# Bias tables of the dilated heads: built one pair ahead on ScalarE and GpSimd, in two buffers

## The reference

```python
DILATED_PATTERNS = ((128, 1), (512, 4), (2048, 16))
slopes = exp2(-8 * arange(1, 9) / 8)                      # head h: 2 ** -(h + 1)
for window, dilation in DILATED_PATTERNS:
    bias = -slopes[:, None, None] * (dilation * abs(delta))[None]
    s = where(mask, q @ k + bias, NEG_INF)
    m = max(s); e = exp(s - m); den = sum(e); num = e @ v
...                                                       # the three patterns are joined by exp(m - max m)
return sum(scale * num) / sum(scale * den)
```

## Time and profile before

| | us |
|---|---|
| median of 3 runs | 3123.47 |
| lowest and highest | 3121.69, 3126.23 |
| the profiled execution | 3126.64 |
| its span (first to last instruction) | 3124.9 |

### The profile page before, as it was taken

One profiled execution on the slowest core, in us unless ns is written; L12 is line 12 of the kernel. 1 busy time (PEld: TensorE's weight loads), 2 busy tenths in 40 slices (PEclk: granted clock), 3 DMA queues, 4 the chain that ended last, 5 costly groups with the idle time before them and its releaser, 6 DMA issues.

```text
span 3124.9 us, 42430 instructions
## 1 busy us (share of the span) xinstructions
PE 2933.4 (94%) x16328; PEld 2234.8 (72%) x16328; DVE 1830.8 (59%) x2574; ACT 915.4 (29%) x1660; POOL 1136.6 (36%) x661
## 2 busy tenths in 40 slices
PE   7999999999999999999999999999998567999998
PEld 6888867677888878887676778887796566555443
DVE  7766685756666676667757566666526985112112
ACT  3222232543222232223235422223236652111111
POOL 3444354454443444442544444443433550000000
PEclk9999999999999999999999999999999688999999
DMA  5222222013222222222200132222230004999998
GB/s 203 95 87 101 81 81 82 2 42 121 84 98 101 81 101 101 95 86 81 108 35 1 68 115 101 91 90 99 81 122 1 21 1 165 414 423 422 424 422 339
DMA packets 44789, 411.47 MB, mean 132 GB/s; under 512 B 4960, under 2 KB 5216, under 8 KB 11744
## 3 DMA queue, kind: packets, MB, share of 16 engines
q1 hardware_dynamic: 44496, 408.03, 33.6%
q0 software_dynamic: 144, 1.38, 0.1%
HBM read 407.29 MB, written 2.10 MB: 131 GB/s over the span
## 4 chain that ended last, share of the span: by engine, by line
PE 78%; DVE 10%; DMA 5%; issue 3%; ACT 3%; POOL 1%; SPq 0%; DVEq 0%; ACTq 0%; POOLq 0%
PE banks L1598 10%; PE banks L1597 10%; PE banks L1596 10%; PE banks L1561 5%; PE banks L1430 5%; PE banks L1869 5%; PE banks L1607 5%; PE banks L1608 5%; PE banks L1609 5%; DMA experts<-moe_w 4%; PE banks L1509 3%; PE banks L1880 2%; PE banks L1645 2%; PE banks L1658 2%; PE banks L1673 2%
## 5 line engine op out<-in xcount | busy, mean ns | idle before, releaser
L784 POOL TENSOR_TENSOR ffn_parts<-ring,ffn_parts 128x2048 fp32r<-128x2048 f32 x87 | 403.0, 4633 | 738.5 <-ACT ffn_parts L887 738.5
L2172 DVE SCALAR_TENSOR_TENSOR x<-banks,x 128x512 f32<-128x512 f32 x704 | 474.3, 690 | 302.2 <-PE banks L1609 301.1
L1598 PE MATMUL banks<-x_parts_high,ffn_parts 128*128 128x512 f32 x672 | 263.9, 393 | 0.0
L1596 PE MATMUL banks<-h_lo,ffn_parts 128*128 128x512 f32 x672 | 263.2, 392 | 0.0
L1597 PE MATMUL banks<-x_parts_high,ffn_parts 128*128 128x512 f32 x672 | 262.9, 391 | 0.0
L1596 PE MATMUL banks<-x_parts_low,ffn_parts 128*128 128x512 f32 x672 | 261.9, 390 | 0.0
L1597 PE MATMUL banks<-h_hi,ffn_parts 128*128 128x512 f32 x672 | 261.9, 390 | 0.0
L1598 PE MATMUL banks<-h_hi,ffn_parts 128*128 128x512 f32 x672 | 261.8, 390 | 0.0
L887 ACT ACTIVATE ffn_parts<-ring 128x2048 fp32r<-128x2048 f32 x88 | 168.5, 1915 | 289.5 <-PE banks L1598 287.8
L789 POOL TENSOR_TENSOR ffn_parts<-ring,ffn_parts 128x1024 fp32r<-128x1024 f32 x88 | 212.8, 2418 | 101.0 <-ACT ffn_parts L893 101.0
L1869 PE MATMUL banks<-experts,mix 128*64 128x256 f32 x1536 | 189.9, 391 | 16.4 <-DMA experts<-moe_w 16.4
(11 more groups left out here) (394 smaller groups left out, 6749.6 us busy)
## 6 DMA issues: line engine op xcount, KB each, us to landing
ring<-ffn_w SPq DMA_DIRECT2D x87, 1536.0 KB, 6.5
experts<-moe_w SPq DMA_DIRECT2D x48, 2048.0 KB, 17.4
experts<-moe_w SPq DMA_DIRECT2D x48, 1024.0 KB, 18.5
ring<-mix_w SPq DMA_DIRECT2D x24, 1536.0 KB, 6.5
ring<-second_w SPq DMA_DIRECT2D x16, 1536.0 KB, 6.5
expert_table<-moe_w SPq DMA_DIRECT2D x16, 1024.0 KB, 15.1
expert_h<-moe_w SPq DMA_DIRECT2D x16, 1024.0 KB, 19.8
expert_table<-moe_w SPq DMA_DIRECT2D x16, 512.0 KB, 13.2
```

Of the source, the lines that this page charges most:

```text
L784: pool.tensor_tensor(s[:, 1], w, s[:, 0].bitcast(F32), ALU.subtract).then_inc(up_split, 1)
L1596: mm(bank[n % 2 + 2 * a], w[:, 0, a, k], lo[:, k], start=k == 0, stop=False)
L1598: last = mm(bank[n % 2 + 2 * a], w[:, 1, a, k], hi[:, k], start=False, stop=k == KC - 1)
L2172: V.scalar_tensor_tensor(x[:, q], bank[4 + q % 4], scale, x[:, q], ALU.mult, ALU.add).then_inc(down_used, c.one(down_used))
```

## The change

DVE no longer builds the tables. `distances` on ACT writes the distance times minus the slope into `HB[n % 2]`, and `counts_added` on POOL adds the log of the count in place. The tables of pair 0 are made before `meet`: by ACT behind its last move out of PSUM, and by POOL behind its last piece of the projection. Those of pair n + 1 are made in the steps of pair n: by ACT behind the exponentials of the second step (a % 4 == 1), by POOL ahead of the products of the third step (a % 4 == 2). DVE waits for `bias_ready` in the first step of a pair. `HB` becomes two buffers, the second one over `h_lo`, which is free there.

```diff
-    HB = view(16384, 2 * 896, a=2)
+    HB = [view(16384, 2 * 896, a=2), nc.alloc_sbuf_tensor_at("bias_odd", [P, 2 * 896], F32, offset=place["h_lo"]).ap().rearrange("p (a n) -> p a n", a=2)]
...
                 u, i = pairs[a // NT], row_of(pairs, a)
+                if u["bias"] is not None and a % NT == 2 and a + NT < NT * len(pairs):
+                    counts_added(a // NT + 1)
                 pool.wait_ge(den_ready, c.next(den_ready))
...
+        def counts_added(n):
+            for e in range(2):
+                pool.wait_ge(bias_scaled, 2 * n + e + 1)
+                pool.tensor_tensor(HB[n % 2][:, e], HB[n % 2][:, e], table[:, C2_MULT:C2_MULT + 896], ALU.add).then_inc(bias_ready, 1)
...
         pool.wait_ge(second_in, 16)
+        counts_added(0)
         meet(pool, c, "pool")
...
+        def distances(pairs, n):
+            for e in range(2):
+                act.activation(HB[n % 2][:, e], table[:, C2_DIST:C2_DIST + 896], ACT.Copy,
+                               scale=-(2.0 ** -(pairs[n]["bias"] + e + 1))).then_inc(bias_scaled, 1)
...
+                if a < steps and pairs[0]["bias"] is not None and a % NT == 1 and a + NT < steps:
+                    distances(pairs, a // NT + 1)
...
         second_inputs(base_second)
+        act.wait_ge(second_in, 16)
+        act.wait_ge(head_sums, 8)
+        distances(dilated_pairs(), 0)
         meet(act, c, "act")
...
                     if a % NT == 0:
-                        for e in range(2):
-                            step(V.scalar_tensor_tensor(HB[:, e], table[:, C2_DIST:C2_DIST + 896], -(2.0 ** -(u["bias"] + e + 1)),
-                                                        table[:, C2_MULT:C2_MULT + 896], ALU.mult, ALU.add))
+                        dve.wait_ge(bias_ready, 2 * (a // NT) + 2)
```

More of the change, by code:

```diff
@@ L254, in program @@
     cmp_ready, cmp_bias, cmp_hid = new("cmp_ready", "cmp_bias", "cmp_hid")
+    bias_scaled, bias_ready = new("bias_scaled", "bias_ready")
     scores_ready, max_ready, probs_ready = new("scores_ready", "max_ready", "probs_ready")
@@ L2235, in maximum @@
                     src = PROBS[:, a % 4]
-                    V.scalar_tensor_tensor(src[:, 0], SCORES[a % 2][:, 0], E_DH ** -0.5, HB[:, 0, at:at + T], ALU.mult, ALU.add)
-                    step(V.scalar_tensor_tensor(src[:, 1], SCORES[a % 2][:, 1], E_DH ** -0.5, HB[:, 1, at:at + T], ALU.mult, ALU.add))
+                    V.scalar_tensor_tensor(src[:, 0], SCORES[a % 2][:, 0], E_DH ** -0.5, HB[a // NT % 2][:, 0, at:at + T], ALU.mult, ALU.add)
+                    step(V.scalar_tensor_tensor(src[:, 1], SCORES[a % 2][:, 1], E_DH ** -0.5, HB[a // NT % 2][:, 1, at:at + T], ALU.mult, ALU.add))
                 else:
```

## The result

The changed kernel takes 3131.38 us (median of 11 executions, 3129.30 to 3135.23), the kernel before 3123.47 us (11 executions beside it, 3121.54 to 3126.23). The ratio is 1.0025, with a 95% interval of 1.0016 to 1.0035: slower by 7.9 us. The ratio itself lies above the 0.2% that can be told from no change, the lower end of its interval (0.16%) does not. The forecast was 3129.6 us in a range of 3126.6 to 3132.8.

What follows compares the result with a forecast made beforehand. The prediction put DVE's table builds on the attention's path, PE carrying 78% of the whole chain of waits. Its terms, 5.02 + 0.65 - 0.17 + 0.65 = +6.15 us, took 3123.47 to 3129.6 us, range 3126.6 to 3132.8.

Steps and rivals of the forecast that it cites:

- Step 1, the start: Attention start: the meeting waits for ACT's copies and POOL's additions; DVE's first scores plus bias come 5.02 us later.
- The half clock of the scores: Attention start: after 5.7 us of idle time, PE's first scores take 2.08 us in place of 1.14.
- the 0.13 taken from the earlier trace: Attention start: the meeting of the engines takes 0.13 us behind the end of POOL's additions.
- Step 2, turns 1 and 2: Turns to pairs 1 and 2: DVE's saved builds become waits for POOL's additions, +0.65 and -0.17 us.
- Step 2, turn 3: Turn to pair 3: DVE waits for POOL's additions and starts at 2401.31 against 2400.66, +0.65 us.
- PE at the end of a wait: Sign at the turns: step 2 is wrong if DVE's idle time is ended by PE or ACT.
- what is pushed back on ACT: Steps 3 and 7: ACT's copies come 1.8 us late, inside DVE's wait, so they cost nothing.
- The costs set at nothing: Attention loop: POOL's delayed products and ACT's delayed work cost nothing; no table load is added.
- B: Rival in the loop: DVE holds up POOL's additions, 2.54 instead of 2.10 us each; sum +8.8 us, chance 0.13.
- C: Rival: PE's clock stays low beyond the first scores, 0.94 us more per step; +7.1 or +8.0 us, chance 0.10.
- D: Rival at the turns: tables are ready in time and the waits vanish; sum -2.8 us, 3120.7 us, chance 0.03.
- E: Rival: the start costs less, with PE's clock still up or additions at 1.73 us; +3.2 to +5.2 us, chance 0.14.

Runs made afterwards that it cites:

- early: Against the changed kernel, ACT's copies for pair 0 stand before its last moves out of PSUM, POOL's additions following them; 3125.51 us, ratio 1.0004.
- dve_turns: Against the changed kernel, only pair 0 is made by ACT and POOL; DVE builds pairs 1 to 3 at the turns; 3129.67 us, ratio 1.0017.
- quarter_dist: The changed kernel with ACT's distances for pairs 2 and 3 cut to 224 of 896 columns, POOL's additions whole; ratio 1.0019.
- quarter_both: The changed kernel with both distances and additions for pairs 2 and 3 cut to 224 of 896 columns; ratio 1.0007.
- dve_idle: Against the kernel before, DVE still builds all tables, but uses the second buffer to place builds where it has time; 3121.70 us, ratio 0.9988.
- quarter_adds: The changed kernel with POOL's additions for pairs 1 to 3 cut to 224 of 896 columns; 3127.74 us, ratio 1.0007.
- dist_sooner: The changed kernel with ACT's distances one step earlier, behind the exponentials of a pair's first step; 3131.06 us, ratio 1.0023.
- again: The changed kernel measured once more as it is; 3131.94 us, ratio 1.0026.
- dve_first: Against the changed kernel, pair 0 is built by DVE behind the meeting as before, the turns as changed; 3126.48 us, ratio 1.0007.
- late_result: Against dve_idle, DVE's low part of a finished output stands one step later, pair 3's builds in steps 9 and 10; 3118.94 us, ratio 0.9981.

## Why the prediction was right, and where its working was off

**Step 1, the start: right to 0.3 us.** Forecast +5.02, measured 7.72 - 2.38 = +5.34. ACT's copies (0.94 each against 0.93) and POOL's additions ended 5.09 us behind A0, where 5.08 had been worked out. That they agree so closely is in part luck: POOL started 0.99 us behind A0 instead of 0.91, and its two additions took 4.10 us instead of 4.17. The half clock of the scores, taken from the long idle time of PE, was there (granted 0.50 over 2358 to 2367). What was short is the meeting: PE's first scores came 2359.53 - 2359.12 = 0.41 us behind POOL's end, against the 0.13 taken from the earlier trace rows, where ACT had come last. In the chain of waits 0.17 us of it lie between POOL's end and its signal and 0.24 on PE; in early, where ACT comes last again, these are 0.04 and 0.09. That row was of another engine, and of a PE that had been idle for 0.65 us and not for 6. dve_turns confirms the term by itself (+5.3 in the trace, +5.2 in the medians), and early that it goes when the work stands sooner.

**Step 2, turns 1 and 2: right.** Forecast +0.65 and -0.17, measured +0.55 and -0.25, both waits ended by POOL (3.07 and 2.27 us). The 2.6 us that DVE was spared came back as waits, as the forecast said.

**Step 2, turn 3: the step that failed.** Forecast +0.65, measured +1.53, with PE and not POOL at the end of the wait. PE at the end of a wait is the sign that the prediction itself had named for its step 2 being wrong. The sentence that failed is the one on what is pushed back on ACT: the two scaled copies "1.8 late" ahead of the copies of the turned probabilities, "again inside the wait of DVE". At full clock they are inside it, by 2404.72 - 2403.97 = 0.75 us. But PE is idle 3.01 us (1.33 before, 1.88 in quarter_dist), its clock falls for the next products and scores, and 0.94 us more of scores and 0.7 of values use up the 0.75 and 0.9 beyond. quarter_dist gives +0.58 for the turn once the copies are short.

**The costs set at nothing.** POOL's products pushed back behind the additions cost nothing, as said: every stretch of steps between the turns has the length of before to 0.01 us. At turn 1 nothing but the additions was as late as 5.66 us, for with short ones it falls to 2.91. No table load was added.

**Rivals.** B, additions held up by DVE, is refuted: two additions take 4.14 or 4.15 us in the loop, beside DVE's work, and 4.10 at the start, where DVE is idle. The Trainium skill, "SBUF — State Buffer", section "SBUF: two separate sides", lets VectorE and GpSimd contend only where VectorE has two SBUF inputs or runs in one of its 2-port modes. The trace agrees as to the two SBUF inputs: with the builds gone POOL's products too are 1.36 us a pair everywhere, none at 2.95. No run here shows the 2-port modes. C is half true: the clock did stay low beyond the first scores (2.08 us for those of step 2, granted 0.50 to 2367), but DVE waited for none of them, and steps 0 to 3 take 8.18 us in both kernels. Its price, 0.94 us for a step's scores, was paid at the third turn. D, tables in time, did not happen; quarter_both shows at turn 2 what it would have given there, 3.14 us instead of 5.13. E did not happen.

**The sum.** +5.34 + 0.55 - 0.25 + 1.53 = +7.2 in the trace against +6.15 forecast; the medians give +7.9, and the interval of the ratio, 5.0 to 10.9 us, holds both. Of the 1.0 us by which the trace lies above the forecast, 0.9 are the third turn, and 0.3 at the start stand against -0.2 at turns 1 and 2. The forecast lay just under the edge of 0.2% (6.25 us) and gave no difference the better chance, 0.51 against 0.47 for slower; the median lies above the edge. Without the extra 0.9 us of turn 3 the trace would give +6.3, which is the edge itself.

What stays open: why the clock fell. It did after 3.00 or 3.01 us of idle time at turn 3 of four kernels, and after 1.33 us in dve_idle (with 0.67 us a little ahead of it). It did not after 2.75 us in quarter_adds, 2.57 in dist_sooner, 1.88 in quarter_dist, or 1.33 in before (with 1.46 a little ahead of it). The last idle time alone does not tell these apart, and none of these kernels was made to.

## What to carry to other kernels

Work that is taken off a busy engine is not cheaper for being on an idle one: ask what stands behind it there, which here was a meeting of all engines (5.3 us) and the release of TensorE (1 us). Moving the work in time on its own engine gave as much as moving it to two other engines (-2.0 against -2.3 us), and more once a wait of that engine was taken away as well (-6.1 against -4.4), and all that it needed of this change was the second buffer. That wait, which had nothing to do with the tables, was worth 2.1 us by itself. A cost "inside a wait" is not yet free: ask whether TensorE is made to idle by it, for in four kernels here the longer idle time went with a fall of the clock that cost 0.9 us more.

## What the runs showed of the chip

- PE's first matmul behind the meeting came 0.13 us behind ACT's end in before, and 0.41 us behind POOL's end in after, again and dve_turns (5.50 us behind A0 in all three). In these three PE had also been idle for 6 us, so it is not shown which of the two made the difference.
- The clock can be lost in the middle of a busy loop: at turn 3 the granted clock fell to 0.50 in after, again, dve_first and early, each time behind 3.00 or 3.01 us in which PE waited for ACT. In after it fell at about 2402, in a stretch where PE was busy without a gap from 2400.78 on.
- GpSimd's addition of two SBUF operands of 896 columns took 2.09 us. The Trainium skill, "GPSIMD Engine Reference", section "Elementwise — side-by-side cycle accounting", gives 4497 ns for 2048 columns, from which 1.97 us had been estimated. The measurement decides.
- Where a build of VectorE and products of GpSimd meet, one alone in a step lengthened only the products (1.07 us for the build, 2.12 for two products, in late_result); two builds in a row beside them took 2.56 us instead of 2.22.
